# Neighbourhood attention: the values held still in TensorE, two heads in column halves, with the inverse sums turned into rows

## What is computed

```python
s_win = einsum(q, k_band) * scale + bias[row distance, column distance]   # -1e30 outside 16 columns
s_ctx = einsum(q, k_ctx) * scale
p = softmax(concatenate([s_win, s_ctx]))
o = einsum(p_win, v_band) + einsum(p_ctx, v_ctx)
# the context tokens themselves, first layer only:
o_c = softmax(q_c @ k_c.T * scale) @ v_c
# then, for every branch i and token n
y = sum_i sigmoid(gate_i) * (branch_i @ w_branch_i)
```

## Time and profile before

| | |
|---|---|
| median of three runs | 3038.85 us (3038.63 to 3039.66) |
| profiled execution, first to last instruction (span) | 3037.7 us, 33914 instructions |
| median less span | 1.15 us |
| TensorE matmul, busy | 2785.5 us, 92% |
| VectorE, ScalarE, GpSimd busy | 1278.1, 929.7, 961.0 us |
| first layer's neighbourhood stage | 1249.56 to 1302.98 |
| second layer's | 2330.19 to 2364.28 |

### The profile page before, as it was taken

How to read it: one execution, slowest core, us unless ns; L and a number is a source line. 1 busy time by engine, 2 the same in 40 slices (tenths; PEclk the granted TensorE clock), 3 DMA queues, 4 the chain that set the end, 5 groups by cost and what they waited for, 6 DMA issues and landing times. The chain is left out here.

```text
span 3037.7 us, 33914 instructions
## 1 busy us (share of the span) xinstructions
PE 2785.5 (92%) x13329; PEld 1865.2 (61%) x13329; DVE 1278.1 (42%) x2372; ACT 929.7 (31%) x1303; POOL 961.0 (32%) x413
## 2 busy tenths in 40 slices
PE   7999999998999998899988999996898998999894
PEld 4877768886876786688764444442675874433331
DVE  5663244244514326753445333323436445332323
ACT  0443333344434223522232222222334342222222
POOL 0166657721873452333210000001363750000000
PEclk9999999998999998999999999998899999999998
DMA  5765875547668233032245999999251567999996
GB/s 182 249 219 180 301 244 178 180 152 250 230 222 292 98 112 122 15 127 93 88 171 234 419 422 422 422 422 367 84 163 43 196 246 300 422 423 422 422 423 269
DMA packets 208912, 746.02 MB, mean 246 GB/s; under 512 B 13876, under 2 KB 15074, under 8 KB 158832
## 3 DMA queue, kind: packets, MB, share of 16 engines
q1 hardware_dynamic: 189872, 669.61, 58.0%
q0 software_dynamic: 18880, 74.22, 7.3%
HBM read 721.00 MB, written 44.27 MB: 252 GB/s over the span
## 5 line engine op out<-in xcount | busy, mean ns | idle before, releaser
L1912 POOL TENSOR_TENSOR weight_ring_r<-weight_ring,weights_high_r 128x2048 fp32r<-128x2048 f32 x126 | 576.5, 4585 | 492.3 <-ACT weights_high_r L1521 412.9
L1521 ACT ACTIVATE weights_high_r<-weight_ring 128x2048 fp32r<-128x2048 f32 x136 | 257.2, 1902 | 608.0 <-PE banks L862 372.7
L857 PE MATMUL banks<-weights_high_r,x_transposed_r 128*128 128x512 f32 x1008 | 397.0, 394 | 11.1 <-ACT weights_high_r L1521 5.5
L2037 POOL DMA_DIRECT2D moe_y<-arena x64 | 34.1, 533 | 921.8 <-DVE arena L2740 921.8
L862 PE MATMUL banks<-weight_ring_r,x_transposed_r 128*128 128x512 f32 x1328 | 324.1, 390 | 1.0 <-POOL weight_ring_r L1912 1.0
L862 PEld LDWEIGHTS banks<-weight_ring_r,x_transposed_r 128*128 128x128 f32 x1328 | 249.8, 188 | 53.8 <-POOL weight_ring_r L1912 1.8
L1912 POOL TENSOR_TENSOR weight_ring_r<-weight_ring,gates_r 128x2048 fp32r<-128x2048 f32 (+1 forms) x52 | 234.7, 4525 | 139.4 <-DVE small L2079 71.9
L857 PEld LDWEIGHTS banks<-weights_high_r,x_transposed_r 128*128 128x128 f32 x1008 | 190.3, 189 | 53.0 <-ACT weights_high_r L1521 6.8
L1762 ACT ACTIVATE arena<-banks 64x1024 f32<-64x1024 f32 x64 | 65.1, 1018 | 501.0 <-PE banks L1255 501.0
L858 PE MATMUL banks<-weights_high_r,arena_r 128*128 128x512 f32 x520 | 202.8, 390 | 0.0
L2725 DVE TENSOR_TENSOR arena<-banks,arena 64x1024 f32<-64x1024 f32 x64 | 78.2, 1222 | 285.4 <-ACT arena L1762 285.4
(11 more groups left out here) (395 smaller groups left out, 4781.6 us busy)
## 6 DMA issues: line engine op xcount, KB each, us to landing
weight_ring<-in_moe_w_up SPq DMA_DIRECT2D x64, 1024.0 KB, 12.7
x_transposed<-in_moe_w_up SPq DMA_DIRECT2D x60, 1024.0 KB, 12.5
tokens_out<-in_moe_w_down SPq DMA_DIRECT2D x60, 1024.0 KB, 14.2
arena<-in_moe_w_gate SPq DMA_DIRECT2D x60, 1024.0 KB, 12.3
weight_ring<-in_moe_w_down SPq DMA_DIRECT2D x60, 1024.0 KB, 15.0
weight_ring<-in_w_in SPq DMA_DIRECT2D x56, 1024.0 KB, 5.2
weights_high<-in_moe_w_gate SPq DMA_DIRECT2D x56, 1024.0 KB, 12.0
weight_ring<-in_ffn_w_in SPq DMA_DIRECT2D x44, 1024.0 KB, 5.3
```

The costliest lines, as they stand in the source:

```text
L857: nc.tensor.matmul(banks[t][:, 0:width], xh, wh[:, k, :], start=k0 + k == 0, stop=False)
L1521: nc.scalar.activation(high(s, kn, width), slot(c, kn, width), ACT.Copy).then_inc(high_ready, 1)
L1912: nc.gpsimd.tensor_tensor(slot(c, kn, width, ring_r), slot(c, kn, width), high(s, kn, width), ALU.subtract).then_inc(low_ready, 1)
L2037: nc.gpsimd.dma_start(ys_dram[e * CAP:(e + 1) * CAP, :], A[own(e), E_Y:E_Y + D]).then_inc(ys_out[e % 2], 16)
```

## The change

1. V product: v is the stationary operand (128 x 64) and 128 columns of transposed probabilities stream. Head 0 goes to columns 0 to 63 of the array and head 1 to columns 64 to 127, in turns; the output has features on the partitions and tokens in the free direction, in one bank (6).
2. The inverses of the sums now have to run along the free direction. VectorE takes the reciprocal, waiting for the exponents, and spreads the two numbers over 64 columns each (`inverse`, a copy SBUF to SBUF, 128 x 128, into `broadcast_row`); TensorE transposes that (bank 7); ScalarE copies it to SBUF (`copy_inverse`); VectorE multiplies the output by it.
3. Order: TensorE does values n-1 in step n, with the transpose of the inverses ahead of it; ScalarE's copy of the inverses of n-1 stands behind its copy of step n; VectorE does `inverse(n)` between `copy_second(n)` and `finish(n-1)`.
4. Branch 2 isn't turned any more. In round 1 VectorE splits it from SBUF (`split_branch`): a cast and a subtraction for each tile.
5. In the code for experts that overflow, three semaphores of VectorE become one.

```diff
@@ tensor: neighbourhood
                 def values(n):
                     j, t = steps[n]
                     k0, nk = na_keys(t)
-                    if n >= 2:
-                        pe.wait_ge(na_out_used, base + n - 1)
+                    pe.wait_ge(inverse_ready, inv + n + 1)
+                    if inv + n > 0:
+                        pe.wait_ge(inverse_copied, inv + n)
+                    nc.tensor.transpose(ps[7][:, 0:P], na_spread(n), ident).then_inc(inverse_turned, 1)
+                    if n >= 1:
+                        pe.wait_ge(na_out_used, base + n)
                     for m in range(2):
                         pe.wait_ge(na_copied[m], base + n + 1)
-                        for k in range(nk):
-                            last = nc.tensor.matmul(ps[6 + n % 2][:, m * 64:m * 64 + 64],
-                                                    na_pT(n, m)[:, k * P:(k + 1) * P], vc[:, k0 + k, 2 * j + m, :],
-                                                    start=k == 0, stop=k == nk - 1)
+                    for k in range(nk):
+                        for m in range(2):
+                            last = nc.tensor.matmul(ps[6][64 * m:64 * m + 64, 0:P], vc[:, k0 + k, 2 * j + m, :],
+                                                    na_pT(n, m)[:, k * P:(k + 1) * P], start=k == 0, stop=k == nk - 1)
                     last.then_inc(na_out, 1)
...
                     turn(n, 1)
-                    values(n)
+                    if n >= 1:
+                        values(n - 1)
+                values(len(steps) - 1)
@@ tensor: rounds of gate and branch products
-                    if n < 2:
+                    if n < 1:
                         turn_branch()
-                    pe.wait_ge(tr_used, branch_turned[b])
+                    if b < 2:
+                        pe.wait_ge(tr_used, branch_turned[b])
+                    else:
+                        pe.wait_ge(rows_split, seen.next(rows_split) if n == 2 else seen.now(rows_split))
@@ scalar: neighbourhood
+                def copy_inverse(n):
+
+                    act.wait_ge(inverse_turned, inv + n + 1)
+                    nc.scalar.activation(na_scale(n), ps[7][:, 0:P], ACT.Copy).then_inc(inverse_copied, 1)
...
                     nc.scalar.activation(na_pT(n, 0)[:, 0:width], ps[4][:, 0:width], ACT.Copy).then_inc(na_copied[0], 1)
+                    if n >= 1:
+                        copy_inverse(n - 1)
+                copy_inverse(len(steps) - 1)
@@ vector: neighbourhood
-                def finish(n):
-                    j, t = steps[n]
+                def inverse(n):
+
+                    dve.wait_ge(na_exp, 2 * (base + n + 1))
                     c = 80 + na_stat(n)
                     v(nc.vector.reciprocal(small[:, c:c + 2], small[:, c:c + 2]))
+                    v(copy(na_spread(n).rearrange("p (m e) -> p m e", m=2), spread(small[:, c:c + 2], 2, 64)), inverse_ready)
+
+                def finish(n):
+
+                    j, t = steps[n]
                     dve.wait_ge(na_out, base + n + 1)
-                    dst = ar(YC + t * 512 + j * 128, 128).rearrange("p (m e) -> p m e", m=2)
-                    v(tt(dst, ps[6 + n % 2][:, 0:128].rearrange("p (m e) -> p m e", m=2), spread(small[:, c:c + 2], 2, 64),
-                         ALU.mult), na_out_used)
+                    dve.wait_ge(inverse_copied, seen.next(inverse_copied))
+                    v(tt(ar(YC + t * 512 + j * P, P), ps[6][:, 0:P], na_scale(n), ALU.mult), na_out_used)
...
                     copy_second(n)
+                    inverse(n)
                     if n >= 1:
                         finish(n - 1)
@@ vector: rounds
+                def split_branch():
+
+                    for t in range(tiles):
+                        dst = A_r[:, YT:YT + 6144].rearrange("p (k t c) -> p k t c", k=12, t=MAX_TILES)[:, 8:12, t, :]
+                        src, low = (a[:, YC + t * 512:YC + (t + 1) * 512].rearrange("p (k c) -> p k c", k=4) for a in (A, A_r))
+                        v(copy(dst, src))
+                        v(tt(low, src, dst, ALU.subtract), rows_split if t == tiles - 1 else dve_step)
...
-                    if n < 2:
-                        branch_parts(n + 1)
+                    if n == 0:
+                        branch_parts(1)
+                    if n == 1:
+                        split_branch()
```

More of the change, by code:

```diff
@@ L278, in build_program @@
         na_out, na_out_used = sem("na_out_ready"), sem("na_out_used")
+        inverse_ready, inverse_turned, inverse_copied = (sem("inverse_" + n) for n in ("ready", "turned", "copied"))
+        rows_split = sem("rows_split")
         spread_ready = sem("expert_slots_marked")
@@ L290, in build_program @@
         gated, halves_ready, summed, y_half = (sem("expert_" + n) for n in ("gated", "halves", "summed", "y_half"))
-        ov = [{n: sem(f"over{i}_{n}") for n in ("marked", "marked_one", "moved", "w_in", "xT", "xT_copied", "gate_up", "halves", "summed", "sigmoid", "gated", "y_half", "hidden",
-                                               "hiddenT", "hiddenT_copied", "down", "y_copied", "y_out")}
+        ov = [{n: sem(f"over{i}_{n}") for n in ("marked", "vector_step", "w_in", "xT", "xT_copied", "gate_up", "halves", "summed",
+                                               "sigmoid", "y_half", "hidden", "hiddenT", "hiddenT_copied", "down", "y_copied", "y_out")}
               for i in range(DEPTH)]
@@ L620, in na_stat, with na_spread, na_scale @@
             return n % 4 * 2
+        def na_spread(n):
+            return brow[:, 256 + n % 2 * P:256 + (n % 2 + 1) * P]
+        def na_scale(n):
+            return brow[:, 512 + n % 2 * P:512 + (n % 2 + 1) * P]
         def wide(units):
@@ L1092, in neighbourhood @@
                 steps, base = na_steps(layer), na_before(layer)
+                inv = seen.now(inverse_ready)
                 def scores(n):
@@ L1134, in neighbourhood @@
                     turn(n, 1)
-                    values(n)
+                    if n >= 1:
+                        values(n - 1)
+                values(len(steps) - 1)
                 pe.wait_ge(na_out_used, base + len(steps))
+                seen.next(inverse_ready, len(steps))
             def dilated():
@@ L1562, in neighbourhood @@
                 steps, base = na_steps(layer), na_before(layer)
+                inv = seen.now(inverse_turned)
+                def copy_inverse(n):
+                    act.wait_ge(inverse_turned, inv + n + 1)
+                    nc.scalar.activation(na_scale(n), ps[7][:, 0:P], ACT.Copy).then_inc(inverse_copied, 1)
                 for n, (j, t) in enumerate(steps):
@@ L1576, in neighbourhood @@
                     nc.scalar.activation(na_pT(n, 0)[:, 0:width], ps[4][:, 0:width], ACT.Copy).then_inc(na_copied[0], 1)
+                    if n >= 1:
+                        copy_inverse(n - 1)
+                copy_inverse(len(steps) - 1)
+                seen.next(inverse_turned, len(steps))
             def dilated():
@@ L2300, in neighbourhood @@
                     copy_second(n)
+                    inverse(n)
                     if n >= 1:
                         finish(n - 1)
-                dve.wait_ge(na_exp, 2 * (base + len(steps)))
                 finish(len(steps) - 1)
@@ L2766, in experts @@
                     dve.wait_ge(xt_ready, b + NE)
+                    steps_ = all_tiles[layer] + 2
                     with dve.Fori(0, n_over) as j:
@@ L2770, in experts @@
                             at = [route[:, OVER_ROWS + k * MAX_TILES + t:OVER_ROWS + k * MAX_TILES + t + 1] for k in range(2)]
-                            ts(slots_, ar(IOTA, CAP), at[0], None, ALU.is_equal).then_inc(over["marked_one"], 1)
-                            dve.wait_ge(over["marked_one"], counted(dve, all_tiles[layer] * j + t + 1))
+                            ts(slots_, ar(IOTA, CAP), at[0], None, ALU.is_equal).then_inc(over["vector_step"], 1)
+                            dve.wait_ge(over["vector_step"], counted(dve, steps_ * j + t + 1))
                             last = stt(slots_, ar(IOTA, CAP), at[1], slots_, ALU.is_equal, ALU.add)
@@ L2776, in experts @@
                         part = route[:, OVER_ROWS:OVER_ROWS + 2 * MAX_TILES]
-                        ts(part, part, -float(CAP), None, ALU.add).then_inc(over["moved"], 1)
-                        dve.wait_ge(over["moved"], j + 1)
+                        ts(part, part, -float(CAP), None, ALU.add).then_inc(over["vector_step"], 1)
+                        dve.wait_ge(over["vector_step"], counted(dve, steps_ * j + steps_ - 1))
                         dve.wait_ge(over["xT"], j + 1)
```

8 lines of the change are left out of this document (4 added, 4 removed).

## The result

The changed kernel takes 3047.15 us (median of 13 runs, 3041.84 to 3050.34), the kernel before beside it 3039.66 (13 runs): a ratio of 1.0027, 95% interval 1.0019 to 1.0034. It is slower, by some 8 us. Predicted were 3040.3 and a range up to 3047.0. The profiled executions stand 7.6 apart (spans 3045.3 and 3037.7).

| stretch | before | after | difference | forecast |
|---|---|---|---|---|
| first layer, stage (first score to first gate product) | 53.48 | 55.13 | +1.65 | +0.6 |
| from there to the turn ahead of the output weight | 201.32 | 204.04 | +2.72 | -1.36 |
| second layer, stage | 34.15 | 37.28 | +3.13 | +3.0 |
| from there to the turn ahead of the output weight | 103.97 | 106.25 | +2.28 | -0.83 |
| everything else | | | -2.2 | 0 |

What follows compares the result with a forecast made beforehand. TensorE, busy almost without gaps in the neighbourhood stages, was taken as the bound. Terms +0.6 (first stage) + 3.0 (second) - 2.2 (branch turn) = +1.4 gave span 3039.1, time 3040.3, range 3031 to 3047.

Steps and rivals of the forecast that it cites:

- The V product: Neighbourhood stages, TensorE: a wide product (four key blocks) falls from 2.11 to 1.15, a narrow one takes 0.73.
- rival 3: V product: column halves don't overlap at 128 columns, a wide product takes 2.3; with stalls +9, 3048; chance 0.1.
- The loop: Stages: ScalarE's copy of the inverses delays the next turn; four steps 11.7 against 12.99, first layer without stalls -4.2.
- VectorE against GpSimd: Stages: GpSimd's subtracts stop VectorE's spread copy; mean 4.8 in the first layer, net +0.6; second layer +3.0.
- the four priced at 4.6: First stage, four stall cases (4.6, 2.4, 7.4, 4.8): 4.6 late if VectorE gets in at the boundary between subtracts.
- sign of failing upward: First layer's stage: clock rows of 0.5 there would show the prediction failing upward.
- The +3.0: Second stage: copies of steps 6 and 7 caught by subtracts; +2.3 with the boundary, +3.8 without, taken as +3.0.
- branch turn: Rounds behind the stages: dropped transposes save 1.66 and 0.83, one caught split instruction loses 0.3; net -2.2.
- a spare pair of banks and over 8 us: Second layer, branch turn: this slack was to absorb a caught split instruction, so no loss was counted there.
- Rivals 1: Stages: the spread copy isn't stopped by GpSimd; first layer -4.2, with the branch -7.7, 3031.2; chance 0.17.
- Rival 2: Both stages: VectorE stands through both subtracts, +4.8, and the granted clock falls; over +6.1, 3045.5; chance 0.2.
- gains 1.5 at most: Second stage: GpSimd's biases set the pace, 5.5 each, so the last row minimum gains 1.5 at most.

Runs made afterwards that it cites:

- the run with the minimum: Changed kernel with the two inverses spread over 64 columns each by a minimum over an axis of length 1, not a copy; 3033.37 against 3037.71, ratio 0.9985.
- the run with the turn kept: Changed kernel with TensorE still doing the third branch's transposes, which nobody reads, while VectorE splits from SBUF; 3041.24 against 3037.38, ratio 1.0012.
- the split in the gap: Changed kernel with the third branch's casts and subtractions moved from round 1 to where VectorE and GpSimd both idle; 3039.51 against 3037.71, ratio 1.0004.
- the early turn of the inverses: Kernel with both edits (split in idle gap, inverses spread by minimum), TensorE transposing the inverses of n-1 before the second turn of n; 3027.49, ratio 0.9970.
- the subtracts later: Changed kernel with GpSimd's two subtracts for the first gate product moved behind the stage, VectorE keeping its copy; one run, 3052.03.

## Why the prediction was wrong

**The V product** was right: 1.09 for the 1.15 forecast, 0.66 for 0.73. Its reason, halves that overlap because they alternate, is half of it for the wide product: without the turns it takes 1.58, not the 2.11 and more of rival 3. **The loop** was right in kind (ScalarE's copy of the inverses precedes each late turn, 0.48 idle ahead of two turns in four) and in size: 11.97 for 11.7, and the first stage without stalls, shown by the run with the minimum, 4.3 shorter for the 4.2 forecast.

**VectorE against GpSimd** in the stages was right in kind: the copies are caught, and VectorE gets in at the boundary. In the first stage the case that came was the one of the four priced at 4.6 (the copies of steps 7 and 8 caught, the first up to the boundary); stalls and lowered clock together cost 54.00 - 49.14 = 4.9 in the run with the turn kept. The sum had no term for the clock. The rows of 0.5 that the prediction named as its sign of failing upward did show in this stage (1280 to 1285), but they are within these 4.9. The changed kernel's own profile has 1.56 more: its first scores ran at half clock (3.55 for 1.99). That is no effect of the change that can be named: of the eleven profiles two have it, the changed kernel's and that of the split in the gap, and the other eight that hold the changed stage in some form don't.

In the second stage the two copies were caught as written, one to the boundary and one to the end. The +3.13 for +3.0 is partly luck. The +3.0 was the middle between +2.3 with the boundary and +3.8 without it; the boundary was there, and the measured end is 0.8 above its case. What stands against each other there is a gain that was put too low (below) and a clock of 0.55 (2360 to 2370) that was put at nothing.

The Trainium skill (SBUF — State Buffer, Who interferes with whom) states that VectorE's copy and cast in a two-port mode meet any GpSimd instruction, that a two-input instruction with both inputs in SBUF meets one that reads SBUF, and that its reductions never do. The 4.50 of the copy, the 4.84 of the cast, the 4.36 of the adder and the flat 0.286 of 24 minima agree.

**The step that failed is the branch turn**, "Net -2.5 + 0.3 = -2.2". The -2.5 is right: 1.77 and 0.86 in the run with the split in the gap. The +0.3 measured +4.5 in the first layer (2.72 + 1.77; 2.9 of it are wait and lateness, 1.6 the half clock behind the wait, by the run with the minimum) and +3.1 in the second (2.28 + 0.86), 7.6 in all. In the first, the prediction followed the caught cast to 1371.6, to the first adder's bank, found 0.3 and stopped there. It left out that an adder with both inputs in SBUF stands behind every tile's multiplication, that the next subtract would meet one of them, and that the turn taken out brings that subtract 1.6 nearer (1374.43 for 1376.05) while VectorE is 0.3 later. In the second, "a spare pair of banks and over 8 us" took one caught instruction for granted where GpSimd subtracts nearly without a break (9.4 + 4.6 + 4.7 + 4.6 between 2400.31 and 2425.8), so that each next SBUF instruction is caught anew.

By the spans the change cost 7.6 where 1.4 was forecast, so the miss is 6.2 (by the medians 3047.15 for 3040.3, 6.9, of which 0.8 is that the kernel before now has 3039.66 for 3038.85). The branch turn alone is 7.2 of it (5.0 for -2.2). The half-clock start added 1.6, the rest of the two stages is 0.4 under its forecast, and what lies outside the four stretches gave 2.2 back: the changed kernel's profile reaches the first stage 1.5 earlier, with the same work ahead of it, and profiles of the same work differ there by more than that (1244.20 to 1252.37). Rivals 1 and 3 fell with the longest copy of 4.50 and the product of 1.09. Rival 2 forecast 3045.5 by starved copies and a lowered clock. The time was near it, and the clock did fall, but VectorE through both subtracts without a boundary didn't occur in either stage, and the loss wasn't there.

The second stage had one more error, hidden by the stalls: "gains 1.5 at most". Without stalls it gained 2.5 (31.66) where the clock held, since behind the last bias the shorter product counts as well, and 1.1 (33.02) where it fell.

## What to carry to other kernels

Before an operand moves from PSUM to SBUF, or an SBUF copy is added on VectorE, list GpSimd's long instructions beside it, and follow a caught instruction through every later instruction of the same kind until VectorE has caught up, not to the first reader. A form that is not stopped can be had for little (0.286 for 0.227), and so can an idle place a few us away. And when work is taken off the bounding engine, redo the timetable of the others behind it: here, with a cast caught already, 1.66 saved on TensorE moved a subtract onto an earlier adder and cost 4.4 (204.04 - 201.35 + 1.66).

## What the runs showed of the hardware

- A reciprocal grows with its columns far faster than a copy: 0.17 for 2, 0.95 for 128, beside 0.286 for a minimum and 0.227 for a copy of the same 128. It isn't stopped by GpSimd's subtracts.
- A TensorE wait can cost more than its length, but didn't always. In the changed kernel 2.25 idle with shorter waits near it was followed by a granted clock of 0.50 over 5 us (1280 to 1285), and 2.21 by 0.66 over 5; with the early turn of the inverses 2.65 was followed by 0.54 over 7. But 2.24 and 2.19 with the minimum alone, and 2.71 in the second stage with the subtracts later, were each followed by 1.00 over the next 4.5 to 5.
- Column halves of 64 with 128 streamed columns: 16 records take 1.09 when the halves alternate and 1.58 when they don't; 8 records take 0.66 and 0.67.
- A VectorE copy that waits for GpSimd got in at the boundary between two subtracts queued one behind the other: in six stages of three kernels such a copy took 4.50, 4.41, 4.20 and three times 1.93, each ending there. The two-input instruction of 11.67 in the earlier trace rows passed two such boundaries.
